# The buffer of low parts of the weights, moved 448 bytes further in SBUF

## The reference

```
x = x + 1/2 * SwiGLU_1(RMSNorm(x))          # w_gate, w_up: 1024 x 2816; w_down: 2816 x 1024
h = RMSNorm(x)
[qA | kA | vA | c_q | c_kv | k_rope | gate_A | gate_B] = h @ w_in
oA = sliding-window attention(qA, kA, vA)    # window 128, sinks, ALiBi, QK-norm
oB = latent attention(c_q @ w_uq, c_kv @ w_ukv, k_rope)
x = x + (sigmoid(gate_A) * oA @ w_branch_a + sigmoid(gate_B) * oB @ w_branch_b) @ w_out
x = x + 1/2 * SwiGLU_2(RMSNorm(x))

def swiglu(x, w_gate, w_up, w_down):
    return (silu(x @ w_gate) * (x @ w_up)) @ w_down
```

## Time and profile before

| | |
|---|---|
| median of 3 runs | 1043.81 us (1042.66 to 1044.01) |
| the profiled execution | 1042.75 us, of it 1041.0 us span |
| PE busy | 1036.3 us in 5648 matmuls |
| PEld busy | 896.0 us in 5648 weight loads |
| DVE busy | 718.0 us |
| ACT busy | 585.8 us |
| granted clock of TensorE | 1.000 |

### The profile page before, as it was taken

How to read it: one execution, slowest core, us unless ns; L and a number is a source line. 1 busy time by engine, 2 the same in 40 slices (tenths; PEclk the granted TensorE clock), 3 DMA queues, 4 the chain that set the end, 5 groups by cost and what they waited for, 6 DMA issues and landing times.

```text
span 1041.0 us, 15559 instructions
## 1 busy us (share of the span) xinstructions
PE 1036.3 (100%) x5648; PEld 896.0 (86%) x5648; DVE 718.0 (69%) x1132; ACT 585.8 (56%) x935; POOL 62.0 (6%) x71
## 2 busy tenths in 40 slices
PE   9999999999999999999999999999999999999998
PEld 8888888998888888888888888889988888888887
DVE  7766676668786866666687666666688868676665
ACT  7545454557964655454565455455678646454552
POOL 0062000121100000000000000001211000000000
PEclk9999999999999999999999999999999999999999
DMA  7765554455335555555545555634454346545541
GB/s 267 257 228 178 201 166 161 145 188 195 132 122 202 182 194 177 211 184 204 182 150 198 197 198 180 210 132 154 150 203 162 122 162 223 201 164 199 192 171 61
DMA packets 35269, 187.53 MB, mean 180 GB/s; under 512 B 4368, under 2 KB 4384, under 8 KB 20128
## 3 DMA queue, kind: packets, MB, share of 16 engines
q1 hardware_dynamic: 34992, 186.51, 51.5%
q0 software_dynamic: 240, 0.53, 0.2%
HBM read 185.98 MB, written 1.05 MB: 180 GB/s over the span
## 4 chain that ended last, share of the span: by engine, by line
PE 99%; DMA 0%; ACT 0%; DVE 0%; issue 0%; ACTq 0%
PE ps L1365 96%; PE ps L1799 1%; PE ps L1389 1%; PE ps L1828 1%; DMA x_cols<-in_x_first 0%; PE ps L1864 0%; PE ps L1708 0%; PE ps L1700 0%; ACT hT L606 0%; PE ps L1410 0%; DVE x_cols L995 0%; ACT w_hi L550 0%; PE ps L1398 0%; ACTq L605 0%
## 5 line engine op out<-in xcount | busy, mean ns | idle before, releaser
L1365 PE MATMUL ps<-hT,w_hi 128*128 128x512 f32 x1408 | 340.9, 391 | 0.2 <-ACT w_hi L550 0.2
L1365 PEld LDWEIGHTS ps<-hT,w_hi 128*128 128x128 f32 x1408 | 259.4, 188 | 50.6 <-ACT w_hi L550 0.4
L880 DVE TENSOR_TENSOR w_lo<-w_raw,w_hi 128x2048 fp32r<-128x2048 f32 x82 | 188.0, 2293 | 87.3 <-ACT w_hi L545 87.3
L1365 PEld LDWEIGHTS ps<-hT,w_lo 128*128 128x128 f32 x1408 | 180.3, 191 | 7.0
L1365 PE MATMUL ps<-hT,w_lo 128*128 128x256 f32 x1408 | 182.3, 283 | 0.0
L1365 PE MATMUL ps<-w_hi,hT 128*128 128x512 f32 (+2 forms) x576 | 174.2, 377 | 0.0
L545 ACT ACTIVATE w_hi<-w_raw 128x2048 fp32r<-128x2048 f32 x85 | 162.0, 1905 | 13.4 <-PE ps L1365 13.2
L1365 PE MATMUL ps<-w_lo,aTh 128*128 128x512 f32 x352 | 137.2, 390 | 0.0
L1365 PE MATMUL ps<-w_hi,aTl 128*128 128x512 f32 x352 | 137.0, 389 | 0.0
L1365 PE MATMUL ps<-w_hi,aTh 128*128 128x512 f32 x352 | 136.8, 390 | 0.0
L574 ACT ACTIVATE S<-ps 128x256 f32<-128x256 f32 x88 | 33.6, 382 | 159.4 <-PE ps L1365 159.4
(11 more groups left out here) (168 smaller groups left out, 953.6 us busy)
## 6 DMA issues: line engine op xcount, KB each, us to landing
w_raw<-in_w_ffn SPq DMA_DIRECT2D x85, 1024.0 KB, 5.0
w_raw<-in_w_ffn SPq DMA_DIRECT2D x90, 512.0 KB, 5.7
w_raw<-in_w_gate SPq DMA_DIRECT2D x16, 1024.0 KB, 5.0
w_raw<-in_w_proj SPq DMA_DIRECT2D x16, 592.0 KB, 4.8
w_raw<-in_w_branch SPq DMA_DIRECT2D x8, 1024.0 KB, 4.8
w_raw<-in_w_out SPq DMA_DIRECT2D x8, 1024.0 KB, 4.8
w_raw<-in_w_uq SPq DMA_DIRECT2D x4, 384.0 KB, 3.0
w_raw<-in_w_ffn SPq DMA_DIRECT2D x4, 256.0 KB, 5.4
```

The lines of the kernel that those rows point to most:

```text
L880: dve.tensor_tensor(wl_gu[b], raw_gu[b], wh_gu[b].bitcast(F32), ALU.subtract).then_inc(lo_gu.sem, 1)
L1365: return pe.matmul(dst, w, m, start=start, stop=stop, skip_group_check=True)
```

## The change

A tensor of 112 columns (448 bytes), which nothing reads or writes, is placed ahead of `w_lo`, and one of 16 columns (64 bytes) behind it. `w_lo` then begins at byte 66,112: 448 bytes further, 64 bytes past a multiple of 512, and 25,024 bytes behind `w_hi` where it was 24,576. It moves as a whole, so its slots for gate and up, for down and for all kinds of the mixing block move alike. Everything behind it is 512 bytes further, and keeps its place modulo 512. `w_raw` and `w_hi` stay. The instructions, their shapes, their order and their waits are the same on every engine.

```
@@ -40,6 +40,7 @@
 MIX_SLOTS = 3
+LO_GAP = 112
 MIX_COLS = {"proj": PROJ_COLS, "gate": GU_COLS, ...}
@@ -107,7 +108,9 @@
         w_raw = sb("w_raw", [P, MIX_SLOTS * GU_COLS])
         w_hi = sb("w_hi", [P, MIX_SLOTS * GU_COLS], F32R)
+        lo_gap = sb("lo_gap", [P, LO_GAP])
         w_lo = sb("w_lo", [P, MIX_SLOTS * GU_COLS], F32R)
+        lo_end = sb("lo_end", [P, 128 - LO_GAP])
```

## The result

The changed kernel takes 1046.73 us (median of 8 runs, 1046.57 to 1048.10), the kernel before 1042.76 us in its 8 runs. The ratio is 1.0038, with a 95% interval of 1.0029 to 1.0047: slower, by 4.0 us, where no change was forecast. One of the four runs of the later experiment e4_rest64 took 4788 us, far outside the other three, and is not counted.

A forecast was written before the change was run, and what follows sets the result against it. TensorE's matmul pitches were taken to bound the kernel. Three terms of 0 us left the 1041.0 us span, plus 1.75 us outside it: 1042.75 us, or 1043.8 us on the runs' median scale; range 1040.5 to 1047.0 us.

The forecast's parts named there:

- What bounds the kernel: Whole kernel: TensorE, busy 1036.3 of 1041.0 us, so the time is the sum of its matmul pitches.
- Term 2 (VectorE): VectorE's writes of `w_lo`: at most 20 ns of 2293 to win, hidden under TensorE; 0.0 us, bounds -1.3 and +1.3.
- term 3 (all others): ScalarE's `w_hi` writes, SyncE's `w_raw` fills and buffers behind `w_lo`: places unchanged or kept modulo 512; 0.0 us.
- Term 1 (TensorE): The 2136 matmuls that read `w_lo`: 0 ns change each, with bounds of 28.4 us less and 3.2 us more.
- The rows nearest to the new place: Transposes reading `x`, 64 bytes past a multiple of 512: 272 ns like those of `S`, taken as grounds for 0.
- Its own sign of being wrong: Matmuls with `w_lo`: any pitch moved by 1 ns or more would show the forecast wrong.
- The slower rival: Loads and streams of `w_lo`: reads starting at odd multiples of 64 bytes cost 1.5 ns, +3.2 us, 1047.0 us; chance 0.11.
- The faster rival: Matmuls with `w_lo`: 13.3 ns is an address-dependent load-stream collision; up to 28.4 us less, 1015.4 us; chance 0.12.
- The much slower rival: VectorE's `w_lo` writes collide with its two reads; at twice the length 64 us more, 1108 us; chance 0.01.
- The 0.76 for no change: Whole kernel: the change does nothing, 1043.8 us, own range 1042.3 to 1045.3; chance 0.76.

The follow-up runs named there:

- e4_rest64: Against the kernel before, everything behind `w_lo` placed 64 bytes further, the weights' buffers staying; 1053.97 us, ratio 1.0106.
- e15_small_after: The changed kernel's layout, with ScalarE and VectorE writing only 64 columns of each weight slot in the SwiGLU loops; 1046.80 us, one run.
- e3_all64: Against the kernel before, all tensors placed 64 bytes further together, so all distances between them stay; 1043.52 us, ratio 1.0002.
- e9_lo256: Against the kernel before, `w_lo` placed 256 bytes further, all else at its place modulo 512; 1043.08 us, ratio 0.9999.
- e7_third_stays: Against the kernel before, only the first two slots of `w_lo` 448 bytes off, the third at its old place modulo 512; 1043.02 us, ratio 0.9996.
- e5_lo128: Against the kernel before, `w_lo` placed 128 bytes further, all else at its place modulo 512; 1049.97 us, ratio 1.0061.
- e6_rest128: Against the kernel before, everything behind `w_lo` placed 128 bytes further, the weights' buffers staying; 1057.14 us, ratio 1.0132.
- e8_rest448: Against the kernel before, everything behind `w_lo` placed 448 bytes further, the weights' buffers staying; 1045.63 us, ratio 1.0022.
- e2_64: Against the kernel before, `w_lo` 64 bytes further (not 448), everything behind it 512 further as in the changed kernel; 1048.50 us, ratio 1.0053.
- e12_ht448: Against the kernel before, only `hT` 448 bytes off, all else at its place modulo 512; 1043.52 us, ratio 1.0005.

## Why the prediction was wrong

**What bounds the kernel** was right: TensorE's pitches are the whole time, and the 3.8 us between the two traces are all in them.

**Term 2 (VectorE) and term 3 (all others)** were right. VectorE's writes are 2293 and 1220 ns, its waits did not grow, and e15_small_after shows that its writes could vanish without a change.

**Term 1 (TensorE) is the step that failed.** It was set to 0 ns on the 2136 matmuls that read `w_lo`. Measured, TensorE took 3.8 us more: those 2136 together 1.3 us less, and the 2864 with `w_hi`, to which the prediction gave no term, 5.3 us more. It failed in three places.

- It priced the place of one operand. "The rows nearest to the new place" were the transposes of `x`, which start at the same 64 bytes modulo 512. e3_all64 shows that the place of an operand is nothing; the distance of the two operands of a matmul is what counts. By distance the nearest row was `oTh`, 256 bytes off, and 256 is exactly the distance that e9_lo256 shows to be the same as 0. The kernel before has no float32r matmul at any distance but 0 modulo 256, so its trace could bound nothing from within. The transposes of `x` do have their operands 64 apart modulo 256 (`ident` starts at 384, `x` at 64) and those of `S` 0 apart, with no difference between them, but they are another kind of matmul: what they tell does not hold for float32r. Their 272 ns are also lengths, not pitches.
- It counted only the matmuls that read `w_lo`. The 1408 high matmuls, which read none of it, lost 2.4 us, and the 704 down matmuls with `w_hi` 1.6 us. e7_third_stays shows the route for the first high pass: a down block in an uneven state hands it on to the next pass. The rows held a sign of this: the high pass behind the low one took 3.65 us for 16, 228.1 ns each, and not 226.7. The prediction averaged it with the down blocks to 227.3 ns, and so took the matmuls of 416 columns for the only ones that are not their columns plus 13.3 ns.
- Its sign was one for all. The 1408 low matmuls won 2.5 us, the others together lost 6.35 us. Its own sign of being wrong, a pitch with `w_lo` that moved by 1 ns or more, was there: 2.2 ns less in the low passes, 2.9 ns more in the down blocks.

**The slower rival** gave 1.5 ns x 2136 = 3.2 us and 1047.0 us, close to the 1046.7 us measured, but by chance: its mechanism, a read that starts at an odd multiple of 64 bytes, is ruled out by e3_all64, and its place, the low matmuls at 121.5 ns, by the trace (117.8 ns). **The faster rival** had the right kind of cause, the load of one operand against the stream of the other. What is now shown is that a few of the 13.3 ns depend on where the two lie to each other. At their best the low passes cost 113.5 ns, 6.8 over their 106.7 ns of columns, and not 13.3. But its period was wrong (128 bytes apart is not like 0, as e5_lo128 and e6_rest128 show, while 256 is), and it took for granted that leaving distance 0 can only help; 64, 128 and 448 all made the down blocks slower. **The much slower rival** did not occur.

The sentence of the Trainium skill that was set against the faster rival, "SBUF — State Buffer", section "SBUF: two separate sides", says of TensorE that it never waits on anyone; "TensorE: Matmul & The Clock Gate", section "Step-by-step: what each phase is for", adds that loading the next weights takes nothing from the running matmul. With respect to VectorE's and ScalarE's writes of the weights e15_small_after agrees (16.612 us a turn against 16.613). With respect to TensorE's own two reads the runs differ by up to 6.3 ns a matmul ((3.832 - 3.631) / 32, e8_rest448 against before, low passes), and the measurement decides.

The range ended at 1047.0 us and held the time, but by luck: its upper end was the price of that slower rival. The 0.76 for no change did not come from the bounds, which were -28 and +3 us: with the new distance absent from every row of float32r, only the transposes of `x` stood behind a peak at 0.

**What stays open.** Why distance 0 costs 13.3 ns, how the load and the stream meet in detail, what makes the low passes keep 113.5 or 117.8 ns at one distance, and whether distances other than 0 repeat after 256 bytes. The runs give the facts, not the mechanism inside.

## What to carry to other kernels

When TensorE bounds a kernel with float32r matmuls, the layout of SBUF is a parameter: what counts is the distance between the operand loaded and the operand streamed, pass by pass (0 and 256 bytes were alike here, and 16 to 128 bytes were not like them). So give each role its own offset and try a few in steps of 16 bytes: here the whole kernel went from 0.9956 to 1.0132 of its time. Read it from start-to-start distances in the timeline, over all passes and not only those that touch what was moved, since a pass hands its state to the next. If the trace has no row with the new relation between two operands, a row with one operand at the new address is no bound for it.

## What the runs showed of the hardware

- The pitch of a float32r matmul depends on the distance between its two operands; 0 and 256 bytes are alike. Over the layouts tried, 256 columns took 113.5 to 120.1 ns on average over a turn and 512 columns of the down blocks 226.7 to 233.3 ns. Moving all tensors together by 64 bytes, `w_lo` by 256, or `w_lo` and everything behind it by 512 changed no pass by more than 0.001 us.
- At one distance a pass can hold either of two pitches (117.8 ns in e2_64, 113.7 ns in e12_ht448).
- After a change of pass the pitch can be uneven for two to nine matmuls (224 to 236 ns for 512 columns in the kernel before and the changed one), or for the whole pass (231 and 236 ns in turn in e8_rest448), in the same pattern in each turn.
- Taking over a third of VectorE's and ScalarE's busy time out of the loop (110.5 to 64.4 us and 88.5 to 50.9 us of 166 us) left every pass of TensorE where it was, to 0.001 us.
- Transfers into SBUF at 423 GB/s or at 9 GB/s made no difference to the first eight low matmuls of a turn.
